# One fused layer on one core: when w_out starts, and how the first expert's products leave PSUM

## The chip, the cores and the metric

One core of a Trainium2 chip runs the whole kernel in one launch. The metric is the device time in microseconds (us). TensorE is PE in the profile, VectorE is DVE, ScalarE is ACT, GpSimd is POOL, and SP issues most of the DMAs.

## The reference

512 tokens with 1024 features go through one layer, all in float32:

```python
h = layer_norm(x)
proj = h @ w_in                       # splits into the inputs of two mixers and two gates
mixed = sigmoid(z_gla) * (gla_branch(...) @ w_gla_proj) + sigmoid(z_fox) * (fox_branch(...) @ w_fox_proj)
h = layer_norm(ALPHA * h + mixed @ w_out)
logits = h @ w_router + b_router      # top 4 of 32 experts for each token, softmax over the four
gu = xb @ w_gate_up[e] + b_gate_up[e] # for the tokens xb of expert e
y = ((clip(up) + 1) * min(gate, 7) * sigmoid(1.702 * gate)) @ w_down[e] + b_down[e]
out = layer_norm(ALPHA * h + sum over the four experts of weight * y)
```

## The kernel before

The work of each engine is one list of instructions written out by hand, with semaphores between the lists. There is no scheduler: an engine that waits holds back all that stands behind it in its list.

Every large product is done in three passes of fp32r matmuls (`passes`, L1694 to L1696): weight and data are each split into a high and a low part, and high x high, high x low and low x high are summed in PSUM. ACT writes the high part of a weight tile (a copy into fp32r), DVE then writes the low part (raw minus high). A weight tile is 128 x 2048 values, 1 MB, and SP loads it with one DMA. Expert weights go through 6 raw buffers and 4 split buffers, tile n of the experts being numbered over all of them: 8 tiles of w_gate_up and 4 of w_down for each expert. SP may load tile n when DVE has split tile n - 6; ACT may split tile n when PE has used tile n - 4; PE may use tile n when DVE has split it.

PSUM has eight banks of 512 columns: `psA` (four) and `psX` (four).

The w_out stage. The last dense product before it, w_fox_proj, has four chunks. A chunk has two halves, each in a bank of `psA`: chunk 38 fills banks 0 and 1, chunk 39 banks 2 and 3. DVE takes each half out with two instructions (L1346, L1347: szf times the bank, added to mix) and counts `dve_half` up; `mix_low` (L1326) writes the low part of mix. After the loop, at L1991, PE waits for all sixteen halves, and then forms `mixed @ w_out` for four token blocks t. Token block t fills two banks, 2(t % 2) and the next. Its four weight tiles j are: j // 2 picks the column half and with it the bank, j % 2 picks which half of the 1024 summed features. Inside t, PE also turns rows of the block before for the router. On DVE `mix_norm(t)` takes the two banks out, adds the residual and normalises; its first instructions also wait for the loads of h and of the norm's gains and offsets, which POOL issues when the dense products are done (L622 to L624).

Routing. Each token block gives a row of lists: `list_row(t)` on DVE (five instructions, L1431 to L1435) writes the places and weights, and `list_tile(t)` on POOL (L647) scatters them with four indirect DMAs into a table in DRAM. When all sixteen have landed, POOL loads the table back (`ltab`, L693); DVE reads it for the first time at L1598, at the end of expert 1. Experts 0 to 3 don't need the table: PE makes their token lists with small matmuls (`table`, L2050), which DVE reads with `take_table`. POOL's queue after the table's load goes on with two loads, the bias rows of expert 2, the gather of expert 3's rows and the scatter of expert 0's results.

Experts. PE's order for expert 0: eight gate-up tiles into all four banks of `psA` (gate in 0 and 1, up in 2 and 3), the bias (`gate_up_bias`, L2105, which raises `gu_done`), and a small table. Then `body(1)`: it waits for `gate_min` and, ahead of bank 2, for `up_ev`, because expert 1's first tile overwrites the same four banks. After tile c = 2 it turns expert 0's activations (`turn_a`), after c = 4 and c = 5 it counts overflow. The down products of expert i - 1 follow the gate-up products of expert i.

DVE's order around it: `swiglu_in(0)` takes the gate banks out with one instruction of 128 x 1024 (L1517), then the up banks with another (L1519); ACT applies Silu; `swiglu_out(0)` (L1525) multiplies. The low parts of expert 1's tiles are written between these: `step_lo(1, c)`.

Of the kernel before, what the change touches and what calls it, by code (L numbers as in the profile page):

```python
# [13 lines left out]
ALU = mybir.AluOpType  # L14
# [8 lines left out]
P = 128  # L23
D = 1024
T = 512
TT = T // P
# [10 lines left out]
LIMIT, SLOPE = 7.0, 1.702  # L37
# [80 lines left out]
def build(nc, a, out):  # L118
# [437 lines left out]
    def _(pool):  # L556
# [86 lines left out]
        def list_tile(t):  # L643

            pool.wait_ge(list_rows, t + 1)
            for k in range(TOPK):
                g.indirect_dma_start(list_dram, bass.IndirectOffsetOnAxis(ap=lidx[:, t, k:k + 1], axis=0),  # L647
                                     lval[:, t, k, :], None, bounds_check=list_bound, oob_is_err=False).then_inc(list_out, 16)

        def gather(tables, turned):  # L650

            if turned is None:
                pool.wait_ge(early_ready, 1)
                pool.wait_ge(lo_ready, NCD + 1)
            else:
                pool.wait_ge(tab_ready, tables)
                pool.wait_ge(xt_done, turned)
            pool.sem_inc(gathers, 1)
            g.indirect_dma_start(xg[:], None, h2_dram, bass.IndirectOffsetOnAxis(ap=gidx[:, 0:1], axis=0),
                                 bounds_check=token_bound, oob_is_err=False).then_inc(xg_in, 16)  # L660
# [22 lines left out]
            g.dma_start(acc_tiles[t], h2[:, t, :]).then_inc(acc_out, 16)  # L683
        pool.wait_ge(list_blank, 16)
        list_tile(0)
        list_tile(1)
        pool.wait_ge(gu_done, 1)
        load_bgu(1)
        gather(3, 2)
        list_tile(2)  # L690
        list_tile(3)
        pool.wait_ge(list_out, 16 * TT * TOPK)
# [66 lines left out]
    def _(act):  # L759
# [280 lines left out]
            s_.copy(dst[:], ps).then_inc(sem, 1)  # L1040

        def silu(i):
            act.wait_ge(gate_min, i + 1)
            s_.activation(act_t[:], gate_t[:], ACT.Silu, scale=SLOPE).then_inc(silu_done, 1)

        def y_evac_over(j, free):
# [95 lines left out]
    def _(dve):  # L1142
# [283 lines left out]
        def list_row(t):  # L1426

            seq.join()
            if t >= 1:
                dve.wait_ge(list_rows, t)  # L1430
            seq.link(v.tensor_tensor(lprod[:], hot[:, t], posm[:, t, 0:E].unsqueeze(1).broadcast_to(shape), ALU.mult))  # L1431
            seq.link(v.tensor_reduce(lpos[:], lprod[:], AX_X, ALU.add))
            seq.mark(v.scalar_tensor_tensor(lidx[:, t, :], lpos[:], float(LE), top_f[:, t, 0:TOPK], ALU.mult, ALU.add))
            seq.link(v.tensor_tensor(lprod[:], hot[:, t], gval[:, t, :].unsqueeze(1).broadcast_to(shape), ALU.mult))
            v.tensor_reduce(lval[:, t, :, 1], lprod[:], AX_X, ALU.add).then_inc(list_rows, 1)  # L1435
# [7 lines left out]
        def step_lo(i, c):  # L1443
            tile_lo(tile_slot(c), tile_no(i, c), c)
# [33 lines left out]
                        ALU.subtract).then_inc(xT_lo_s, 1)  # L1478
        tile_lo(2, 2, 2)
        tile_lo(3, 3, 3)  # L1480
        list_row(1)
        seq.mark(weigh(3))
        seq.join()
        v.tensor_copy(gate_s[:], gate_s[:]).then_inc(vals_ready, 1)
# [8 lines left out]
        def take_table(x, chain):  # L1493

            dve.wait_ge(tab_done, x + 1)
            chain.mark(v.tensor_reduce(queue[:, 3, 1:2], psD[:, 0, 2:4], AX_X, ALU.add))
            if isinstance(x, int) and x <= 1:
                chain.join()
                v.tensor_copy(queue[:, 3, 0:1], psD[:, 0, 0:1]).then_inc(tab_ready, 1)
                dve.wait_ge(tab_ready, x + 1)  # L1500
                return
            dve.wait_ge(xg_in, 16 * (x - 1))
            chain.link(v.tensor_copy(queue[:, 3, 0:1], psD[:, 0, 0:1]))
            chain.mark(v.tensor_scalar(didx[:], queue[:, 0, 0:1], BIG, None, ALU.add))
            v.tensor_scalar(gidx[:], psD[:, 0, 0:1], BIG, None, ALU.add).then_inc(tab_ready, 1)
# [9 lines left out]
        def swiglu_in(i):  # L1515
# [3 lines left out]
            v.tensor_scalar(by_pair(up_t), psA[:, 2:4, :].rearrange("t b (q p k) -> t (b q) k p", p=P, k=2), LIMIT,  # L1519
                            -LIMIT, ALU.min, ALU.max).then_inc(up_ev, 1)  # L1520

        def swiglu_out(i):
            dve.wait_ge(silu_done, i + 1)
            dve.wait_ge(up_ev, i + 1)
            v.scalar_tensor_tensor(act_t[:], up_t[:], 1.0, act_t[:], ALU.add, ALU.mult).then_inc(act_ready, 1)  # L1525
# [6 lines left out]
        tile_lo(0, 6, 6)  # L1532
        tile_lo(1, 7, 7)
        take_table(1, seq)
        for b in range(3):
            ins = v.tensor_copy(member3[:, :, b * E:(b + 1) * E], member[:])
        ins.then_inc(counts_in, 1)
        step_lo(1, 0)
        turned_lo(xT_hi_s, 2, xT1_hi, xT1_lo, xT_lo_s)
        shift_queue(seq)  # L1540
        step_lo(1, 1)
        swiglu_in(0)
        step_lo(1, 2)
        take_table(2, seq)
        swiglu_out(0)
        step_lo(1, 3)
        list_row(2)
        list_row(3)
        seq.join()
        start = seq.used  # L1550

# [136 lines left out]
    def _(pe):  # L1688
# [299 lines left out]
            if t == TT - 1:  # L1988
                ins.then_inc(xt_done, 1)

        pe.wait_ge(dve_half, 2 * (NCD - NPROJ))  # L1991
        pe.wait_ge(wo_lo_s, 4)
        for t in range(TT):
            if t >= 2:
                pe.wait_ge(wo_evac, 2 * (t - 1))
            for j in range(4):
                hi = wo_high(j).rearrange("p (k c) -> p k c", k=HK)
                lo = raw_lo[:, (NCD + j) % RAW, :].rearrange("p (k c) -> p k c", k=HK)
                dst = psA[:, 2 * (t % 2) + j // 2, :]
                for kk in range(HK):  # L2000
                    k = HK * (j % 2) + kk
                    if t == 0 and j < 2:
                        pe.wait_ge(mix_lo_s, k + 1)
                    tok = slice(t * P, (t + 1) * P)
                    ins = passes(dst, (mix_hi[:, k, tok], mix_lo[:, k, tok]), (hi[:, kk, :], lo[:, kk, :]),
                                 k == 0, k == KT - 1)
                if j % 2 == 1:
                    ins.then_inc(wo_done, 1)
                if j == 0 and t >= 2:
                    turn_logits(t - 2)  # L2010
                if j == 2 and t >= 1:
                    turn_h2(t - 1, 0)
                    turn_h2(t - 1, 1)
                if j == 1 and t == 2:
                    positions(0)
                if j == 2 and t == TT - 1:
                    positions(1)
            if t >= 1:
                route(t - 1)
# [54 lines left out]
        def gate_up(n, c, parts, after_first=False):  # L2074

            tile_ready(n)
            hi, lo = xsplit(c)
            for b in range(4):
                if after_first and b == 2:
                    pe.wait_ge(up_ev, 1)  # L2080
                cols = slice(b * 512, (b + 1) * 512)
                ins = passes(psA[:, b, :], (parts[0][:, c, :], parts[1][:, c, :]), (hi[:, cols], lo[:, cols]), c == 0,
                             False)
            ins.then_inc(tile_used, 1)
# [68 lines left out]
        gate_up_bias(0)  # L2153
        pe.wait_ge(tab_ready, 2)
        table(2, 2)

        def body(i):
            first = isinstance(i, int) and i == 1
            second = isinstance(i, int) and i == 2
            split_ready(xT_hi_s, xT_lo_s, i + 1)  # L2160
            if first:
                pe.wait_ge(gate_min, 1)
            else:
                pe.wait_ge(up_ev, i)
            for c in range(GUC):
                gate_up(tile_no(i, c), c, (xT1_hi, xT1_lo) if first else (xT_hi, xT_lo), first and c == 0)
                if first:
                    if c == 2:
                        turn_a(0, 1)
                    if c == 4:  # L2170
                        overflow_counts()
                    if c == 5:
                        overflow_ranks()
                if c == GUC - 2:
                    if first:
                        overflow_list()
                        pe.wait_ge(tab_ready, i + 2)
                        table(i + 2, bass.ds(i + 2, 1))
                if second and c == 3:
                    pe.wait_ge(bd_in, 64)  # L2180
                    pe.wait_ge(tab_ready, 4)
                    pe.wait_ge(y_ready, 1)
                    split_ready(aT_hi_s, aT_lo_s, 2)
                    gate_bias(0)
                if second and c == 5:
                    pe.wait_ge(stage_ready, TT)
                    gate_bias(1)
            gate_up_bias(i)
            if second:
                pe.wait_ge(stage_ready, 2 * TT)  # L2190
            split_ready(aT_hi_s, aT_lo_s, i)
            turn_x(i + 1)
            if first:
                pe.wait_ge(tab_ready, i + 3)
                pe.wait_ge(routed, 1)
            else:
                pe.wait_ge(y_ready, i - 1)
            for q in range(DNC):
                down(tile_no(i, GUC + q), GUC + q, q)
            turn_a(i, i + 1)  # L2200
# [61 lines left out]
```

## Time and profile before

| | us |
|---|---|
| median of 3 runs | 1767.01 |
| lowest, highest of the 3 | 1764.19, 1767.33 |
| the profiled execution | 1764.92 |
| its span | 1763.3 |

| engine | busy, us | share of the span |
|---|---|---|
| PE | 1728.7 | 98% |
| DVE | 1342.0 | 76% |
| ACT | 1114.0 | 63% |
| POOL | 286.3 | 16% |

Times in the rows are us from the start of the span. In a row of the timeline the number in square brackets is how long the engine had been idle before the instruction, with the instruction that ended the wait. Neighbouring instructions of one engine overlap a little, so what one costs in a full queue is the distance from its start to the next start.

### The profile page before, as it was taken

To read this page: it belongs to the slowest core of one execution; us is meant where nothing else is said; L and a number is where in the kernel's file an instruction comes from. 1 tells how busy PE (TensorE), PEld (TensorE's weight loads), DVE (VectorE), ACT (ScalarE), POOL (GpSimd) and SP (SyncE) were. 2 spreads that over 40 slices of the span, in tenths; PEclk is the share of its full clock that TensorE was granted. 3 is DMA by queue.
4 is the path that set the end of the run, shared out by engine and by line. 5 is a ranking of instruction groups with operands and counts; after the bars stand their busy time and mean duration, and the time that the engine had idled before them with its cause. 6 is when DMAs were issued, how large, how long until landed. Compare 5 with 4: busy or idle time off the path is not lost. (4 is left out here: it accounts for less than half of the span.)

```text
span 1763.3 us, 23505 instructions
## 1 busy us (share of the span) xinstructions
PE 1728.7 (98%) x8305; PEld 1408.9 (80%) x8306; DVE 1342.0 (76%) x1172; ACT 1114.0 (63%) x946; POOL 286.3 (16%) x227
## 2 busy tenths in 40 slices
PE   9999999999999999999999999999999999999995
PEld 6777888888887777888788888888888888888884
DVE  6323324333356899998999999999999999999998
ACT  5534334463222567777777777777777777777775
POOL 3000000000001252221212121212121212122211
PEclk9999999999999999999999999999999999999997
DMA  8322322122332699999999999999999999999994
GB/s 295 95 91 72 87 81 67 54 72 88 104 119 97 226 351 385 356 380 379 375 376 377 370 382 374 368 377 385 367 374 380 386 364 371 388 385 362 366 379 165
DMA packets 115697, 487.98 MB, mean 277 GB/s; under 512 B 18912, under 2 KB 49632, under 8 KB 66497
## 3 DMA queue, kind: packets, MB, share of 16 engines
q1 hardware_dynamic: 99576, 455.76, 67.1%
q0 software_dynamic: 16064, 31.55, 6.4%
q8 instruction: 32, 0.52, 0.1%
q14 instruction: 17, 0.13, 0.0%
q10 hardware_dynamic: 8, 0.01, 0.0%
HBM read 476.22 MB, written 28.36 MB: 286 GB/s over the span
## 5 line engine op out<-in xcount | busy, mean ns | idle before, releaser
L1441 DVE TENSOR_TENSOR wlo<-raw,whi 128x2048 fp32r<-128x2048 f32 x382 | 863.3, 2288 | 65.3 <-ACT whi L988 64.2
L988 ACT CAST whi<-raw 128x2048 fp32r<-128x2048 f32 x382 | 724.7, 1913 | 202.3 <-PE psA L1696 165.7
L1694 PE MATMUL psA<-whi,xT_hi 128*128 128x512 f32 x1036 | 408.1, 394 | 2.3 <-issue 2.3
L1695 PE MATMUL psA<-wlo,xT_hi 128*128 128x512 f32 x1036 | 404.3, 390 | 0.0
L1696 PE MATMUL psA<-whi,xT_lo 128*128 128x512 f32 x1036 | 404.2, 390 | 0.0
L1694 PEld LDWEIGHTS psA<-whi,xT_hi 128*128 128x128 f32 x1036 | 195.2, 188 | 43.5 <-issue 4.2
L1696 PEld LDWEIGHTS psA<-whi,xT_lo 128*128 128x128 f32 x1036 | 195.2, 188 | 40.9
L1695 PEld LDWEIGHTS psA<-wlo,xT_hi 128*128 128x128 f32 x1036 | 195.4, 189 | 39.3
L1694 PE MATMUL psX<-whi,aT_hi 128*128 128x512 f32 x496 | 195.8, 395 | 0.0
L1696 PE MATMUL psX<-whi,aT_lo 128*128 128x512 f32 x496 | 193.4, 390 | 0.0
L1695 PE MATMUL psX<-wlo,aT_hi 128*128 128x512 f32 x496 | 193.3, 390 | 0.0
L1162 DVE TENSOR_TENSOR wlo<-raw,whi 128x2048 fp32r<-128x2048 f32 x40 | 92.5, 2311 | 121.4 <-ACT whi L769 121.3
L1694 PE MATMUL psA<-hT_hi,whi 128*128 128x512 f32 x416 | 164.5, 395 | 0.0
L670 POOL DMA_INDIRECT acc_dram<-y_t,didx x31 | 103.5, 3337 | 364.5 <-ACT y_t L1055 279.1
L1696 PE MATMUL psA<-hT_hi,wlo 128*128 128x512 f32 x416 | 162.1, 390 | 0.0
L1695 PE MATMUL psA<-hT_lo,whi 128*128 128x512 f32 x352 | 137.1, 389 | 0.0
L675 POOL DMA_DIRECT2D bgu<-bgu_dram x64 | 38.8, 609 | 480.2 <-PE psA L2105 476.9
L769 ACT CAST whi<-raw 128x2048 fp32r<-128x2048 f32 x40 | 76.5, 1912 | 59.3 <-PE psA L1696 58.6
L1696 PEld LDWEIGHTS psX<-whi,aT_lo 128*128 128x128 f32 x496 | 93.1, 188 | 19.5
L1694 PEld LDWEIGHTS psX<-whi,aT_hi 128*128 128x128 f32 x496 | 93.2, 188 | 18.6 <-issue 0.2
L1695 PEld LDWEIGHTS psX<-wlo,aT_hi 128*128 128x128 f32 x496 | 93.2, 188 | 18.5
L1694 PEld LDWEIGHTS psA<-hT_hi,whi 128*128 128x128 f32 x416 | 78.1, 188 | 17.1 <-issue 1.8
(393 smaller groups left out, 2008.0 us busy)
## 6 DMA issues: line engine op xcount, KB each, us to landing
raw<-in_w_gate_up SPq DMA_DIRECT2D x254, 1024.0 KB, 8.9
raw<-in_w_down SPq DMA_DIRECT2D x128, 1024.0 KB, 8.3
raw<-in_w_in SPq DMA_DIRECT2D x32, 1024.0 KB, 5.4
raw<-in_w_gla_proj SPq DMA_DIRECT2D x4, 1024.0 KB, 5.1
raw<-in_w_fox_proj SPq DMA_DIRECT2D x4, 1024.0 KB, 5.1
raw<-in_w_out SPq DMA_DIRECT2D x4, 1024.0 KB, 5.0
xt<-in_x SPq DMA_DIRECT2D x4, 512.0 KB, 7.1
h_dram<-xt POOLq DMA_DIRECT2D x4, 512.0 KB, 6.1
```

The lines of the kernel that those rows point to most:

```text
L670: g.indirect_dma_start(acc_dram, bass.IndirectOffsetOnAxis(ap=didx[:, 0:1], axis=0), y_t[:], None, bounds_check=token_bound, oob_is_err=Fa ...
L675: g.dma_start(bgu[part:P:32, :], bgu_rows[part, e, :].rearrange("(n c) -> n c", c=512)).then_inc(bgu_in, 16)
L769: s_.copy(whi[:, c % SPL, :], raw[:, c % RAW, :]).then_inc(hi_ready, 1)
L988: s_.copy(xsplit(c)[0], xraw(slot)).then_inc(hi_ready, 1)
L1162: v.tensor_tensor(wlo[:, c % SPL, :], raw[:, c % RAW, :], whi[:, c % SPL, :].bitcast(F32), ALU.subtract).then_inc(lo_ready, 1)
L1441: v.tensor_tensor(lo, xraw(slot), hi.bitcast(F32), ALU.subtract).then_inc(lo_ready, 1)
L1694: mm(dst, sh, mh, start=first, stop=False)
L1695: mm(dst, sh, ml, start=False, stop=False)
L1696: return mm(dst, sl, mh, start=False, stop=last)
```

## The change

Five edits:

1. In the w_out stage PE waits for 14 of the 16 halves before token block 0 (the two of chunk 38 and all before them) and for all 16 before token block 1, and takes block 0's weight tiles in the order j = 0, 2, 1, 3.
2. Expert 0's products leave PSUM by banks: `first_in` takes the place of `swiglu_in(0)`, with four instructions of one bank each. PE's first tile of expert 1 waits for each bank by itself. Silu's count is moved by the two additional signals.
3. `first_in` stands ahead of `step_lo(1, 1)`, where `swiglu_in(0)` stood behind it.
4. `list_row(1)` goes from ahead of `weigh(3)` to the other two list rows, behind `step_lo(1, 3)`; POOL's `list_tile(1)` goes behind the gather of expert 2's rows. The three copies into `member3` go from ahead of `step_lo(1, 0)` to behind `take_table(2)`.
5. PE does four 128 x 128 matmuls of ones behind the table ahead of `body(1)`.

```diff
-        list_tile(1)
         pool.wait_ge(gu_done, 1)
         load_bgu(1)
         gather(3, 2)
+        list_tile(1)
         list_tile(2)
         list_tile(3)
...
-            act.wait_ge(gate_min, i + 1)
+            act.wait_ge(gate_min, 2 if isinstance(i, int) and i == 0 else i + 3)
...
         tile_lo(3, 3, 3)
-        list_row(1)
         seq.mark(weigh(3))
...
+        def first_in():
+
+            dve.wait_ge(gu_done, 1)
+            for b in range(4):
+                src = psA[:, b, :].rearrange("t (q p k) -> t q k p", p=P, k=2)
+                dst = by_pair((gate_t, up_t)[b // 2])[:, 2 * (b % 2):2 * (b % 2) + 2]
+                if b < 2:
+                    v.tensor_scalar(dst, src, LIMIT, None, ALU.min).then_inc(gate_min, 1)
+                elif b == 2:
+                    v.tensor_scalar(dst, src, LIMIT, -LIMIT, ALU.min, ALU.max).then_inc(gate_min, 1)
+                else:
+                    v.tensor_scalar(dst, src, LIMIT, -LIMIT, ALU.min, ALU.max).then_inc(up_ev, 1)
...
         take_table(1, seq)
+        step_lo(1, 0)
+        turned_lo(xT_hi_s, 2, xT1_hi, xT1_lo, xT_lo_s)
+        shift_queue(seq)
+        first_in()
+        step_lo(1, 1)
+        step_lo(1, 2)
+        take_table(2, seq)
         for b in range(3):
             ins = v.tensor_copy(member3[:, :, b * E:(b + 1) * E], member[:])
         ins.then_inc(counts_in, 1)
-        step_lo(1, 0)
-        turned_lo(xT_hi_s, 2, xT1_hi, xT1_lo, xT_lo_s)
-        shift_queue(seq)
-        step_lo(1, 1)
-        swiglu_in(0)
-        step_lo(1, 2)
-        take_table(2, seq)
         swiglu_out(0)
         step_lo(1, 3)
-        list_row(2)
-        list_row(3)
+        for t in range(1, TT):
+            list_row(t)
         seq.join()
...
-        pe.wait_ge(dve_half, 2 * (NCD - NPROJ))
+        pe.wait_ge(dve_half, 2 * (NCD - NPROJ) - 2)
         pe.wait_ge(wo_lo_s, 4)
         for t in range(TT):
+            if t == 1:
+                pe.wait_ge(dve_half, 2 * (NCD - NPROJ))
...
-            for j in range(4):
+            for j in (0, 2, 1, 3) if t == 0 else range(4):
...
-                if after_first and b == 2:
+                if after_first and b == 3:
                     pe.wait_ge(up_ev, 1)
+                elif after_first:
+                    pe.wait_ge(gate_min, b + 1)
...
         table(2, 2)
+        for _ in range(4):
+            mm(psX[:, 1, 2 * P:3 * P], ones[:], ones[:], start=True, stop=True)
...
-            if first:
-                pe.wait_ge(gate_min, 1)
-            else:
+            if not first:
                 pe.wait_ge(up_ev, i)
```

## Rows read from the trace of the kernel before

**Rows 1.** The page, part 1: busy us, share of the span, instructions.

```profile
PE 1728.7 (98%) x8305; PEld 1408.9 (80%) x8306; DVE 1342.0 (76%) x1172; ACT 1114.0 (63%) x946; POOL 286.3 (16%) x227
```

**Rows 2.** Waits of PE: instruction, releaser, us in total, times, longest.

```profile
PE psA L1694 <- issue: 2.3, 2, 1.9
```

**Rows 3.** Windows: length, busy of each engine, granted clock, DMA share, GB/s.

```profile
540.00:542.00 2.00, 0.49 (x4) 0.07 (x2) 1.45 (x3) 0.06 (x2) 0.92 (x2) 1.00 0.00 0
631.00:633.20 2.20, 0.31 (x3) 0.22 (x2) 2.20 (x3) 2.18 (x2) 1.22 (x2) 0.81 1.11 362
633.20:639.20 6.00, 5.97 (x14) 4.74 (x15) 5.97 (x8) 1.90 (x3) 1.24 (x1) 0.50 0.98 351
840.00:876.00 36.00, 34.55 (x160) 28.28 (x158) 32.61 (x21) 26.29 (x17) 10.00 (x5) 1.00 1.01 377
```

**Rows 4.** Timeline where w_out starts: start, us, engine, line, operation.

```profile
535.76 2.29 DVE L1337 TENSOR_TENSOR raw_lo<-raw,wlo 128x2048 fp32r<-128x2048 f32 x1
...
540.10 0.39 PE L1696 MATMUL psA<-hT_hi,wlo 128*128 128x512 f32 x1
...
541.85 1.46 DVE L1326 TENSOR_TENSOR mix_lo<-mix,mix_hi 128x512 fp32r<-128x512 f32 x2
...
541.99 0.50 PE L1694 MATMUL psA<-whi,mix_hi 128*128 128x512 f32 x1 [1.51 <-DVE mix L1347]
```

**Rows 5.** Timeline, DVE's first normalised block and PE's turn of it.

```profile
558.02 0.75 DVE L1388 SCALAR_TENSOR_TENSOR h<-h,small,lnmix_b 128x512 f32<-128x512 f32 x1
...
561.17 1.03 PE L1947 MATMUL psX<-ident,h 128*128 128x128 f32 x8
```

**Rows 6.** Timeline of PE: expert 0's bias, its table, tile c = 4 of expert 1.

```profile
630.26 0.51 PE L2105 MATMUL psA<-bgu,ones_r 2*128 2x512 f32 x4
630.70 0.61 PE L2050 MATMUL psX<-vals,slots 128*128 128x4 f32 x4
...
647.89 0.39 PE L1694 MATMUL psA<-whi,xT_hi 128*128 128x512 f32 x1
```

**Rows 7.** Timeline of DVE from expert 0's last tiles to expert 1's c = 5.

```profile
625.07 0.68 DVE L1536 COPY member<-member 128x128 f32<-128x128 f32 x3
...
629.59 2.29 DVE L1441 TENSOR_TENSOR wlo<-raw,whi 128x2048 fp32r<-128x2048 f32 x1
631.80 1.22 DVE L1517 TENSOR_SCALAR gate_t<-psA 128x1024 f32<-128x1024 f32 x1
...
636.27 0.15 DVE L1496 TENSOR_REDUCE small<-psX 128x1 f32<-128x2 f32 x1
...
636.66 1.22 DVE L1525 SCALAR_TENSOR_TENSOR act_t<-up_t,act_t 128x1024 f32<-128x1024 f32 x1
637.79 2.28 DVE L1441 TENSOR_TENSOR wlo<-raw,whi 128x2048 fp32r<-128x2048 f32 x1
639.99 0.28 DVE L1431 TENSOR_TENSOR lprod<-hot,posm 128x128 f32<-128x128 f32 x1
...
642.67 0.86 DVE L1469 TENSOR_SCALAR slots<-iota,posm 128x128 fp32r<-128x128 f32 x4
...
647.39 1.22 DVE L1510 TENSOR_TENSOR aT_lo<-psX,aT_hi 128x1024 fp32r<-128x1024 f32 x1 [1.66 <-ACT aT_hi L1040]
```

**Rows 8.** Timeline: POOL's list writes and the table's load; DVE's first use.

```profile
641.60 1.05 POOL L647 DMA_INDIRECT list_dram<-lval,lidx  x1 [2.77 <-DVE lval L1435]
...
662.23 0.60 POOL L693 DMA_DIRECT2D ltab<-list_dram  x1 [5.85 <-DMA list_dram<-lval,lidx]
...
680.96 0.17 DVE L1598 CAST lrows<-ltab 128x34 uint32<-128x34 f32 x1
```

**Rows 9.** DMA issues of 640 to 680: count, KB each, median us to landing.

```profile
list_dram<-lval,lidx POOLq DMA_INDIRECT x8, 5.6
ltab<-list_dram POOLq DMA_DIRECT2D x1, 34.0 KB, 6.1
```

**Rows 10.** The same of 605 to 630.

```profile
list_dram<-lval,lidx POOLq DMA_INDIRECT x8, 13.0
```

## The prediction

> **What bounds the kernel now.** I read the busy shares of the page first, then the waits of PE, then windows of a few microseconds around the two places that the change touches, then the timelines there. PE is busy 1728.7 of 1763.3 us [rows 1]: whatever doesn't change when PE works changes nothing. The waits of PE give the few places where it is late [rows 2]. The windows price two of them [rows 3]. From 540 to 542 PE is busy 0.49 of 2.00 us, at full clock. From 631.0 to 633.2 it is busy 0.31 of 2.20 us, and inside that stretch the granted clock begins to fall (0.81, which is 0.84 us at half rate); the next 6.00 us stand at 0.50, that is 1.2 in place of 2.4 GHz, and hold 14 matmuls. At full clock the timeline has matmul starts 0.227 us apart (a tile of 12 is 2.72 us), so 14 take 3.2 us, and the slow stretch costs 2.8 us. Behind it PE stands at 36 of 36 us in most windows, so a microsecond gained or lost at 640 reaches the end. One exception: from 840 to 876 PE lacks some 1.45 us at a DMA share of 1.01 [rows 3]. DMA is full there, but its transfers are released by PE's own progress, six tiles ahead, so an earlier PE starts them earlier; I take this stretch as unchanged.
>
> **The start of w_out.** Before, PE's last matmul of the dense products starts at 540.10 and the first of w_out at 541.99, released by mix at L1347 [rows 4]; the natural next start is 540.33. What PE still needs is there: the last low part of w_out's tiles ends at 538.05, and banks 0 and 1 were emptied for chunk 38, one chunk of 10.9 us earlier. Tiles j = 0 and j = 2 need only the first four parts of mix; 24 matmuls take until 545.8, and the last two low parts of mix end at 543.31 [rows 4]. Saved: 541.99 - 540.33 = 1.66 us. What is late next? Bank 0 of block 0 is now done after 36 matmuls and not 24, at 548.5, but DVE starts that block only when the norm's inputs have come, which is later still. The turn of block 0 on PE moves from 561.17 to 559.51, and DVE starts the second half of that block at 558.02 for 0.75 us, so ends at 558.77 [rows 5]: 0.7 us of cover, and each microsecond by which those inputs come later than here costs one beyond it. From there on all stages up to expert 0's end wait for PE, so they move with it. The bounds of this edit are 0 and -1.66; I take **-1.66**. The times below are those of the old trace, without this shift.
>
> **PSUM by banks.** The bias starts at 630.26 and takes 0.51 [rows 6], so `gu_done` stands at about 630.8. Before, DVE was then in `step_lo(1, 1)` (629.59) and came to the gate banks at 631.80 [rows 7]. Now it comes early: without `list_row(1)` (1.34 us: two rows lie between 639.99 and 642.67) and the member copies (0.7) it is ready at about 627.6, and waits over 3 us for the bias. A bank of 512 columns isn't in the trace of before for this operation; half of 1.22 us is the lower bound, the whole of it the upper, and I take 0.62, next to half, as DVE's rows scale with columns. Gate bank 0 is free at 631.5, the four at 633.3; PE uses a bank for 0.68 us, so it never catches up with DVE inside this tile. The table ends at 631.3 [rows 6], the four ones take 4 x 0.11 (eight 128-column turns take 1.03 [rows 5], with the last one's drain), so PE starts tile 8 at 631.75 in place of 633.2. That is 1.5 us, and with no long gap the clock most likely stays up here, another 2.8.
>
> **But DVE is next, and it loses what PE gains.** In front of tile c = 1 stands `step_lo(1, 1)`, which formerly was done before the evacuation and now comes behind it. DVE's queue, each cost as start to start [rows 7]: four banks to 633.3; c = 1 (2.21, from 629.59 to 631.80) to 635.5; c = 2 to 637.7; the four small table instructions (0.39, 636.27 to 636.66) to 638.1; the member copies, newly here (0.6 to 0.7), to 638.7; `swiglu_out` (1.13) to 639.9; c = 3 (2.2) to 642.1; three list rows where there were two (3 x 1.34 = 4.0) to 646.1; slots (0.8) to 646.9; c = 4 (2.2) to 649.1. PE: c = 0 until 634.5, waits 1.0, c = 1 from 635.55, c = 2 until 641.0, the turn until 641.8, c = 3 from 642.1 to 644.8. Then it waits **4.3 us** for c = 4 and starts it at 649.1. Before, it started c = 4 at 647.89 [rows 6]. So at c = 4 PE is 1.2 us later than before, although it left expert 0 1.5 us earlier and ran at full clock. The reason is the DVE work moved into this stretch: 2.2 + 0.7 + 1.34 = 4.2 us more, +0.2 for two more instructions, less 0.95 of earlier start, less the 1.66 us that DVE formerly waited at aT_lo [rows 7]. That wait is gone, and the low parts of c = 5 follow 3.3 us behind those of c = 4, just PE's own pace with its count. **+1.2**; bounds +0.5 (banks at half cost, every start-to-start a little less) and +1.8 (without a slow clock DVE, now late by 1.7, is also last at expert 1's act_t).
>
> **The clock in the new gap.** PE idle for 1.0 us of 631.0 to 632.4 and hardly loaded just before was enough here for the fall; 1.5 us at 540.5 were not [rows 3, 4]. A gap of 4.3 us is longer than either. The cost: before, the low clock stayed for 6.0 us after PE had resumed, and lost 2.8. If it begins about 1 us into the gap and lasts as long as before, 0.84 + 6.0 = 6.8 us in all, 3.6 us of work at half rate remain, losing 1.7. Nothing covers it, as DVE by then is no longer ahead of PE nor behind it. Between 0 (no fall) and 3.6 (a fall only at the end of the gap) I take **+2.3**, between the two that come from the row of the slow stretch.
>
> The Trainium skill (TensorE: Matmul & The Clock Gate, "Loop structure matters more than you think") says that a copy out of PSUM by DVE between two groups of matmuls leaves PE warm. This trace disagrees: the clock fell during just such a copy, 0.81 in 631.0 to 633.2 and then 0.50. By that rule there would be no fall in either kernel's evacuation; the gap here is at a tile's low part, about which the sentence says nothing.
>
> **Sum.** 1764.92 (the profiled execution; span 1763.3 and 1.6 around it) - 1.66 + 1.2 + 2.3 = 1766.8. That execution lies 2.1 us below the median of the runs, 1767.01; the same change on the median gives 1768.9. The four times of before average 1765.9, which gives 1767.7. I forecast **1768**: no change that a measurement can tell, leaning to slower.
>
> **Lists on POOL: the rival on the slower side.** Instead of eight list writes behind the gather there are twelve, and the first now waits for DVE at 643.5. Eight took from 641.60 to 656.4 [rows 8], 1.85 each, so twelve end at 665.9. POOL then waits for the landings: 5.85 us before [rows 8] gives 671.8; with the 13.0 of the earlier burst [rows 10] it is 678.9. The table's load lands 6.1 later [rows 9]: 677.9 or 685.0. DVE wants it at L1598, 680.96 before [rows 8], now about 682 to 685, and I estimate a tile, some 2.5 us, that PE has in hand there. Behind the load in POOL's queue stand expert 2's bias rows, expert 3's gather and expert 0's scatter, which start 10 to 17 us later than before, all of them needed only when PE is at the end of expert 2. It decides from a landing at about 686 on, and then costs one for one: with writes of 2.1 us and landings of 13 us the table comes at 690 or 691, +4 to +5, so 1771 on the profiled execution and 1773 on the median. For it: the bursts are as slow as that under full DMA. Against: DMA is less full from 642 to 655.
>
> The Trainium skill (DMA: Bandwidth & Descriptors, "Anatomy of one DMA — SWDGE (gpsimd) path") gives about 2 us of fixed cost for a DMA from GpSimd. The trace shows medians of 5.6 and 13.0 us for these list writes [rows 9, 10], so it disagrees. By the page's figure the table would be back by about 671, an estimate, and this rival would have no chance; the measured rows leave it one.
>
> **It does what it says.** If DVE kept up, PE would be at c = 4 at 631.75 + 10.9 + 0.8 = 643.45 and not 647.89: -4.4, with -1.66 it is -6.1, 1758.8 on the profiled execution and 1761 on the median. Against it stands only the sum of DVE's queue, but that has no free stretch: c = 4's low part would have to end 5.6 us before my figure.
>
> **No fall of the clock.** Then only the stalls count: -1.66 + 1.7 = 0, the time of before, 1765 to 1767. For it: the fall in the trace needed more than a gap of 1.5 us, and PE works at full rate before and behind this gap. Against: 4.3 us.
>
> **Chances.** The forecast 0.55, lists late 0.15, as it says 0.08, no fall 0.18, the rest 0.04 for something that I don't see. A measurement of this kernel tells about 0.2%, 3.5 us, from no change. Slower by more than that: the lists and the upper part of the forecast (fall late, or counted from the low runs), 0.27. Faster: 0.09. Within: 0.64. The range 1763 to 1773.5 holds the forecast with both ends of the clock's cost, no fall, and the lists up to +5; it leaves out "as it says".
>
> **What would show it.** w_out's first matmul follows the last dense one by 0.23 us. DVE waits 3 us for PE ahead of `first_in`; four instructions of 0.65 us each; the clock stays at 1.00 from 631 to 640 (less the shift). PE waits about 1.0 us for wlo ahead of c = 1 and over 4 us ahead of c = 4, with the clock at 0.50 behind it. POOL loads the table at 672 or later, without a wait of DVE at L1598. I am wrong if PE reaches c = 4 of expert 1 without that gap, or if the clock stays up through it.

## The result, and the profile after

| | before | after |
|---|---|---|
| median of 22 runs each, us | 1763.85 | 1766.83 |
| lowest to highest | 1762.51 to 1767.33 | 1765.35 to 1769.16 |
| the profiled execution (span) | 1764.92 (1763.3) | 1766.36 (1764.8) |

The ratio of after to before is 1.0016, with a 95% interval of 1.0010 to 1.0022: the change makes the kernel 1.8 to 3.9 us slower. The medians differ by 3.0 us, less than the 0.2% (3.5 us) that the prediction took for the least that a measurement can tell, but with 22 runs each it is outside noise. The first three runs of before (median 1767.01) were high ones; with 22 its median is 1763.85.

The waits of PE in the kernel after (instruction, releaser, us in total, times, longest). Compare [rows 2]:

```profile
PE psA L1706 <- DVE wlo L1441: 4.8, 2, 4.1
PE psX L1713 <- DVE act_t L1537: 1.9, 2, 1.1
...
PE psA L1706 <- issue: 0.3, 1, 0.3
```

The 1.9 us ahead of expert 1 and the wait for mix are gone. (The 0.3 us of "issue" lie behind 900 us; before has the same 0.3 there.) Between 625 and 675 PE now waits for nothing but the new releaser on top: the low part of a weight tile, `wlo`, twice, once for 4.1 us. The windows around those places, columns as in [rows 3]:

```profile
541.00:543.00 2.00, 2.00 (x11) 1.65 (x10) 1.42 (x4) 0.09 (x1) 0.87 (x2) 1.00 0.00 0
629.50:633.00 3.50, 3.50 (x24) 2.96 (x24) 2.87 (x5) 3.31 (x3) 1.22 (x2) 1.00 1.04 377
644.20:648.40 4.20, 0.08 (x1) 0.02 (x1) 4.10 (x11) 1.90 (x1) 3.59 (x3) 0.84 0.44 176
648.40:653.60 5.20, 5.19 (x12) 4.06 (x13) 5.20 (x3) 0.00 (x0) 4.89 (x2) 0.50 0.76 240
840.00:876.00 36.00, 35.29 (x166) 28.78 (x165) 32.63 (x19) 26.21 (x16) 9.09 (x5) 1.00 1.01 378
```

PE is full where w_out starts and where expert 1 starts, at full clock. It is empty from 644.2 to 648.4, and there the granted clock falls to the 1.2 GHz level; the 12 matmuls behind it take 5.2 us at 0.50. Two gaps of before were closed and a larger one was opened behind them.

The start of w_out and the turn of the first block (answers to [rows 4, 5]):

```profile
541.15 0.39 PE L1708 MATMUL psA<-hT_hi,wlo 128*128 128x512 f32 x1
541.38 0.39 PE L1706 MATMUL psA<-whi,mix_hi 128*128 128x512 f32 x1
...
559.19 0.75 DVE L1388 SCALAR_TENSOR_TENSOR h<-h,small,lnmix_b 128x512 f32<-128x512 f32 x1
560.42 1.03 PE L1959 MATMUL psX<-ident,h 128*128 128x128 f32 x8
```

PE between the experts, with the tile that waits (answers to [rows 6]):

```profile
629.50 0.51 PE L2121 MATMUL psA<-bgu,ones_r 2*128 2x512 f32 x4
629.94 0.61 PE L2064 MATMUL psX<-vals,slots 128*128 128x4 f32 x4
630.41 1.14 PE L2173 MATMUL psX<-ones 128*128 128x128 f32 x8
631.30 0.48 PE L1706 MATMUL psA<-whi,xT_hi 128*128 128x512 f32 x1
...
648.41 0.76 PE L1706 MATMUL psA<-whi,xT_hi 128*128 128x512 f32 x1 [4.13 <-DVE wlo L1441]
```

DVE's queue meanwhile (answers to [rows 7]). It waits 3.17 us for the bias and is then without a pause until the low part of c = 4 is done, 645.99 + 2.28:

```profile
630.13 1.29 DVE L1528 TENSOR_SCALAR gate_t<-psA 128x512 f32<-128x512 f32 x2 [3.17 <-PE psA L2121]
...
632.53 4.48 DVE L1441 TENSOR_TENSOR wlo<-raw,whi 128x2048 fp32r<-128x2048 f32 x2
...
637.32 0.49 DVE L1555 COPY member<-member 128x128 f32<-128x128 f32 x3
637.73 1.22 DVE L1537 SCALAR_TENSOR_TENSOR act_t<-up_t,act_t 128x1024 f32<-128x1024 f32 x1
638.87 2.28 DVE L1441 TENSOR_TENSOR wlo<-raw,whi 128x2048 fp32r<-128x2048 f32 x1
641.07 0.28 DVE L1431 TENSOR_TENSOR lprod<-hot,posm 128x128 f32<-128x128 f32 x1
...
645.18 0.88 DVE L1469 TENSOR_SCALAR slots<-iota,posm 128x128 fp32r<-128x128 f32 x4
645.99 2.28 DVE L1441 TENSOR_TENSOR wlo<-raw,whi 128x2048 fp32r<-128x2048 f32 x1
```

POOL's list writes, the table's load and DVE's first use of it (answers to [rows 8, 9]):

```profile
642.68 1.05 POOL L647 DMA_INDIRECT list_dram<-lval,lidx  x1 [2.77 <-DVE lval L1435]
...
672.09 0.98 POOL L647 DMA_INDIRECT list_dram<-lval,lidx  x1 [0.30 <-issue]
676.22 0.60 POOL L693 DMA_DIRECT2D ltab<-list_dram  x1 [3.15 <-DMA list_dram<-lval,lidx]
```

```profile
683.49 0.17 DVE L1610 CAST lrows<-ltab 128x34 uint32<-128x34 f32 x1
```

And the landings of 640 to 680, with the columns of [rows 9]:

```profile
list_dram<-lval,lidx POOLq DMA_INDIRECT x12, 5.1
ltab<-list_dram POOLq DMA_DIRECT2D x1, 34.0 KB, 4.1
```

To follow where time goes, I use one table for all kernels. Its columns are distances of PE's bias rows (L2105 before, L2121 after) in each one's profiled execution: expert 0 to expert 1 (the stretch of the change), 1 to 2, and 2 to 8. Undisturbed, an expert takes 35.02 us, so the last column is 210.1 when PE never waits there. "Clock low" is how long the granted clock was 0.50 between 625 and 660.

| kernel | median, us | ratio to before, interval | bias 0 to 1 | 1 to 2 | 2 to 8 | clock low |
|---|---|---|---|---|---|---|
| before | 1763.85 | 1 | 30.47 | 38.04 | 213.5 | 6.8 |
| after | 1766.83 | 1.0016 (1.0010 to 1.0022) | 34.37 | 37.61 | 212.4 | 6.8 |
| e1_w_out_alone | 1761.76 | 0.9987 (0.9978 to 0.9996) | 29.00 | 38.03 | 212.4 | 3.4 |
| e1b_wait_alone | 1762.94 | 0.9994 (0.9985 to 1.0003) | 28.50 | 38.19 | 213.8 | 0 |
| e2_expert_part_alone | 1768.48 | 1.0021 (1.0012 to 1.0030) | 34.23 | 37.61 | 213.1 | 6.8 |
| e6_old_queue_order | 1761.88 | 0.9985 (0.9976 to 0.9994) | 28.69 | 38.19 | 213.8 | 0 |
| e5b_old_order_no_ones | 1762.24 | 0.9995 (0.9986 to 1.0005) | 28.73 | 38.17 | 212.6 | 0 |
| e3_lo_ahead_of_banks | 1763.79 | 1.0001 (0.9992 to 1.0010) | 29.59 | 38.36 | 216.5 | 0 |
| e11_row1_back | 1764.36 | 1.0003 (0.9994 to 1.0012) | 31.95 | 37.61 | 214.0 | 3.4 |
| e9_ones_in_the_gap | 1767.16 | 1.0017 (1.0008 to 1.0026) | 34.63 | 37.61 | 212.2 | 0 |
| e9b_half_the_ones | 1765.52 | 1.0011 (1.0002 to 1.0020) | 31.87 | 38.59 | 212.7 | 0 |
| e8_member_on_act | 1761.29 | 0.9986 (0.9977 to 0.9995) | 28.13 | 38.17 | 211.9 | 0 |
| e10_before_bias_spread | 1761.63 | 0.9990 (0.9981 to 0.9999) | 28.53 | 38.19 | 210.1 | 0 |
| e12_all_gains | 1758.28 | 0.9966 (0.9954 to 0.9978) | 28.14 | 38.17 | 210.1 | 0 |

The medians of before beside the experiments were 1763.4 to 1764.1.

### The profile page after: what moved, and what is told of

It is laid out like the page before. It is cut to its first block, busy times and chain, and to the rows that moved or that the text cites. A ratio compares the mean times of both kernels' runs of the same rounds, so it can differ in the third digit from the quotient of the medians.

```text
span 1764.8 us, 23552 instructions
## 1 busy us (share of the span) xinstructions
PE 1729.7 (98%) x8313; PEld 1410.7 (80%) x8314; DVE 1342.3 (76%) x1174; ACT 1113.8 (63%) x946; POOL 291.0 (16%) x227
## 4 chain that ended last, share of the span: by engine, by line
PE 90%; DVE 4%; ACT 2%; DMA 2%; issue 2%; POOLq 0%; SPq 0%; DVEq 0%; ACTq 0%
PE psA L1706 21%; PE psA L1708 21%; PE psA L1707 21%; PE psX L1706 6%; PE psX L1708 6%; PE psX L1707 6%; PE psX L1713 3%; DVE wlo L1441 1%; DMA raw<-in_w_down 1%; PE psX L1900 1%; PE psX L1885 1%; ACT whi L988 1%; PE psA L2121 1%; PE psX L1909 0%; DMA raw<-in_w_in 0%
```

## The experiments

**The two halves of the change.** First each alone: w_out's three edits on the kernel before, and the change without them.

```diff
-        pe.wait_ge(dve_half, 2 * (NCD - NPROJ))
+        pe.wait_ge(dve_half, 2 * (NCD - NPROJ) - 2)
         pe.wait_ge(wo_lo_s, 4)
         for t in range(TT):
+            if t == 1:
+                pe.wait_ge(dve_half, 2 * (NCD - NPROJ))
...
-            for j in range(4):
+            for j in (0, 2, 1, 3) if t == 0 else range(4):
```

> The kernel before with the w_out part of the change alone (14 halves, order 0, 2, 1, 3). Theory (the stages behind wait for PE, so the start of w_out reaches the end whole): the first w_out matmul 0.23 us behind the last dense one, expert 0's bias 1.7 us earlier, -1.7 us in all, ratio 0.9990. Rival (the norm's inputs or the routing chain take it back): 0, ratio 1.000.

> The change without its w_out part. Theory: DVE's moved work makes PE wait over 4 us for the low part of c = 4, and the clock falls in that gap; from expert 0's bias to expert 1's bias 34.4 us in place of 30.5, in all +3 to +4.5 us, ratio 1.0017 to 1.0025. Rival (the slowdown comes from w_out starting earlier, which shifts everything against the DMAs): 0 or faster.

Measured 0.9987 and 1.0021, both near what was expected: by these ratios w_out's part gains about 2.3 us and the expert part loses about 3.7 us; by the medians beside those of before in the same session (1763.83) it is 2.1 and 4.6. The product of the ratios, 1.0008, lies a little under the 1.0016 of both together, by no more than their intervals allow; the medians add up to 2.6 of 3.0 us. From the last low part of mix to expert 0's bias it takes 87.6 to 87.7 us with the old start and 85.8 to 85.9 with the new one: 1.8 us, and all of it reaches the bias. One profiled execution with the new start, that of e3, takes 87.5: there the granted clock was 0.50 from 598.8 to 602.0, in a stretch where the code is the same in all kernels and no other profile has a fall. So the loss is in the expert part.

**Is the order of the tiles needed?** The same without the last of the three edits.

> The kernel before with PE's earlier start of w_out (14 halves ahead of block 0, 16 ahead of block 1) in the old tile order 0, 1, 2, 3. Theory (the order isn't needed: tile j = 1 comes 2.7 us behind the start, and its first low part is there, each of the others 0.68 us later): the same 1.7 us as with the new order, ratio 0.9987 to 0.9990. Rival (j = 1 reaches the last parts of mix too early and waits): up to 0.5 us less gain.

From mix to the bias it is 85.85 us, the same as with the new order. The waiting edit is the whole gain in the trace. The measured 0.9994 is compatible with 0.9987, and with no change; this run alone would not show the gain.

**The old order of the queues around the evacuation by banks.** The changed kernel with DVE's and POOL's lists as before:

```diff
+        for b in range(3):
+            ins = v.tensor_copy(member3[:, :, b * E:(b + 1) * E], member[:])
+        ins.then_inc(counts_in, 1)
         step_lo(1, 0)
         turned_lo(xT_hi_s, 2, xT1_hi, xT1_lo, xT_lo_s)
         shift_queue(seq)
+        step_lo(1, 1)
         first_in()
-        step_lo(1, 1)
         step_lo(1, 2)
         take_table(2, seq)
-        for b in range(3):
-            ins = v.tensor_copy(member3[:, :, b * E:(b + 1) * E], member[:])
-        ins.then_inc(counts_in, 1)
         swiglu_out(0)
         step_lo(1, 3)
-        for t in range(1, TT):
-            list_row(t)
+        list_row(2)
+        list_row(3)
...
         tile_lo(3, 3, 3)
+        list_row(1)
         seq.mark(weigh(3))
...
         list_tile(0)
+        list_tile(1)
         pool.wait_ge(gu_done, 1)
         load_bgu(1)
         gather(3, 2)
-        list_tile(1)
```

> The changed kernel with DVE's and POOL's old order around it: list row 1, its list writes, the member copies and the low part of c = 1 stand where they stood before, all ahead of the evacuation by banks. Theory (the 4.2 us of moved DVE work are the loss): DVE comes to the banks 0.95 us behind the bias, PE starts expert 1 at about 632.5 on the old axis, waits about 1.8 us ahead of c = 4 and starts it 1.9 us earlier than in the kernel before; with w_out's 1.7 it is -3.3 us against before, ratio 0.998, and up to 3 us less if the clock stays up. Rival (four small instructions and bank waits are what costs): still slower than before, ratio over 1.000.

Measured 0.9985, 1.9 us under before by the medians: faster than before, as the theory has it, but by less than the 3.3 us expected, although the clock stayed up in the profile. PE's waits from 625 to 675 in this kernel:

```profile
PE psA L1707 <- DVE wlo L1441: 1.3, 1, 1.3
PE psX L1714 <- DVE act_t L1538: 0.4, 1, 0.4
PE psA L1707 <- DVE gate_t L1529: 0.3, 1, 0.3
```

The gap of 4.1 us is gone with nothing changed but the places of DVE and POOL instructions, so the four small instructions and the waits by bank are not the loss. But the second thing that this run shows is against me: expert 0 to 1 takes 28.69 us, and the old evacuation takes 28.50 and 28.53 where the clock happened to stay up (e1b, e10). In these traces taking the banks out one by one gains nothing even in the better order, and the medians of this kernel and of e1, 1761.88 and 1761.76 in one session, say the same. The 1.9 us ahead of expert 1 were DVE being late, not the size of its instruction; with banks PE starts earlier and waits the same time a few tiles later.

**Single moved terms.** The low part of c = 1 alone put ahead of `first_in()`, and list row 1 with its list writes alone put back.

> The changed kernel with the low part of expert 1's c = 1 again ahead of the evacuation by banks, in the 3.2 us in which DVE waits for the bias; list rows, list writes and member copies stay late. Theory (DVE's queue in this stretch is a plain sum, of which this is the largest moved term, 2.2 us): PE doesn't wait ahead of c = 1, and the gap ahead of c = 4 shrinks from 4.5 to about 2.7 us; 2.2 us under the changed kernel, ratio 1.0004, and 2.5 lower still where the clock stays up. Rival (the list rows alone make the gap): less than 0.5 us, ratio 1.0015.

> The changed kernel with list row 1 and its list writes back in their old places, nothing else. Theory (a plain sum): DVE's wait ahead of the banks shrinks from 3.2 to 1.8 us, the gap ahead of c = 4 from 4.5 to 3.2 us, 1.4 us under the changed kernel, ratio 1.0008. Rival (what matters is twelve list writes in one burst on POOL): much more than 1.4 us.

The waits of PE from 625 to 675, e3 first and e11 second:

```profile
PE psA L1706 <- DVE wlo L1441: 2.8, 1, 2.8
```

```profile
PE psA L1707 <- DVE wlo L1441: 3.3, 2, 2.7
```

Of the two waits of e11 one is the 0.6 us ahead of c = 1, as after. The wait ahead of c = 4 went from 4.1 to 2.8 and 2.7 us, where I expected 2.7 and 3.2 (with the 0.2 us between two starts). The medians fell by 3.0 and 2.5 us, where I expected 2.2 (more if the clock stays up) and 1.4. In the traces expert 0 to 1 is 4.8 and 2.4 us shorter: 2.2 and 1.4 from the queue, the rest from a fall of the clock that is gone in e3 and half as long in e11. A plain sum over DVE's queue fits, and e11's 2.5 us need no cost of the twelve list writes of their own. The profiled execution of e3 took 1768.0, the upper end of its runs, with the fall of the clock at 598.8 and 216.5 us from expert 2 to 8; its median is 1763.79.

**What the clock costs.** PE was given matmuls of ones inside the gap:

```diff
             for c in range(GUC):
+                if first and c == 4:
+                    for _ in range(32):
+                        mm(psX[:, 1, 2 * P:3 * P], ones[:], ones[:], start=True, stop=True)
```

> The changed kernel with 32 more 128 x 128 matmuls of ones on PE between c = 3 and c = 4 of expert 1, into an unused stretch of PSUM: some 3.5 us of work inside the gap of 4.5 us. Theory (the fall of the clock in the gap costs 2.3 to 2.8 us of its own): the granted clock stays at 1.00 there and the time is 2.5 us under the changed kernel, ratio to before about 1.000. Rival (the slow stretch is covered by DVE's queue): no difference from the changed kernel, 1.0016.

The time was that of the changed kernel, 1.0017. That was not the rival, but my size: the 32 lasted 7.3 us, and c = 4 started at 651.50 in place of 648.41. The clock stayed up. So with 16:

> As the kernel with ones in the gap, but with 16 matmuls: in the earlier run each 128 x 128 float32 matmul took two passes, 0.23 us, so that 32 of them lasted 7.3 us and pushed c = 4 back by 3.1 us, as much as the clock gave. 16 take 3.6 us, inside the gap of 4.5. Theory (the fall costs 2.5 us by itself): the clock stays at 1.00, c = 4 starts when its low part is done, 2.5 us under the changed kernel, ratio 1.0002. Rival (DVE's queue covers the slow stretch): 1.0016 as before.

Windows of that kernel, the old gap and what follows it:

```profile
644.20:647.60 3.40, 3.40 (x32) 3.35 (x31) 3.33 (x9) 1.90 (x1) 2.79 (x3) 1.00 0.38 153
648.30:653.60 5.30, 5.30 (x28) 4.45 (x29) 5.30 (x3) 1.92 (x1) 5.00 (x2) 1.00 0.72 229
```

5.3 us now hold 28 matmuls where 5.2 held 12. Expert 0 to 1 falls from 34.37 to 31.87, 2.5 us, the price of the fall where it happens. But 1 to 2 rises from 37.61 to 38.59: PE comes to the turn of act_t and to expert 2 ahead of DVE and waits there, 0.3 and 0.4 us, where the changed kernel doesn't wait between 660 and 700. Net 1.5 us in the traces, 1.3 in the medians. Both theories were half right: the fall has a price of its own, and DVE's queue takes back part of it.

**Do the four ones ahead of expert 1 keep the clock up?** The kernel with the old queue order, without them:

> The kernel with the old queue order and the evacuation by banks, without the four matmuls of ones ahead of expert 1. Theory A (the ones keep the clock up): the gap behind the table grows from 0.3 to 1.2 us and the clock falls in it, for 3.4 to 6.8 us as in the kernels without ones; 1.4 to 2.8 us over the kernel with ones, less 1.3 us that DVE's wait ahead of c = 4 hides, so ratio to before 0.9988 to 0.999. Theory B (a gap of 1.2 us is short enough): no fall, same time as with ones, 0.9985, or 0.1 us less.

No fall, with PE empty for 1.4 us, and 28.73 us from expert 0 to 1 against 28.69. In this one trace theory B holds. It is not shown for the kernel: the intervals of 0.9995 and 0.9985 overlap, but each execution, profiled or not, also has a mean granted clock, rounded to 0.001 (0.001 is 3.5 us at the low level), and it is 0.995 in ten of the eleven executions with the ones and in five of the eleven without them. Theory A may hold in some executions. In the kernels with the old evacuation, whose wait of 1.9 us is the same in all four, the fall came in two of four profiled executions: 6.8 us in before, 3.4 in e1, none in e1b and e10. Windows of two of these, the wait and what follows it, e1 first, then e1b. (The Trainium skill, TensorE: Matmul & The Clock Gate, "Loop structure matters more than you think", says that a copy out of PSUM leaves PE warm, in a loop whose next matmuls follow at once. Here PE waited 1.9 us for the copy, and it stayed warm in two of these four and not in two.)

```profile
630.70:632.60 1.90, 0.03 (x1) 0.06 (x1) 1.90 (x3) 1.88 (x2) 1.00 (x2) 0.85 1.07 347
632.60:635.40 2.80, 2.80 (x7) 2.22 (x8) 2.80 (x2) 1.47 (x2) 0.00 (x0) 0.50 0.98 232
```

```profile
630.20:632.00 1.80, 0.00 (x0) 0.01 (x1) 1.80 (x3) 1.78 (x2) 0.95 (x2) 1.00 1.04 402
632.00:638.00 6.00, 5.98 (x26) 4.98 (x27) 5.97 (x8) 3.60 (x4) 1.24 (x1) 1.00 1.00 325
```

**Taking work out of DVE's queue, and the waits between 800 and 912.** The first kernel is that of the old queue order, with the member copies on ACT:

```diff
         turned_hi(xt_done, 2, xT1_hi, xT_hi_s)
-        for c in range(1, XSPL):
-            step_hi(1, c)
+        step_hi(1, 1)
+        step_hi(1, 2)
+        act.wait_ge(mem_ready, TT)
+        for b in range(3):
+            ins = s_.copy(member3[:, :, b * E:(b + 1) * E], member[:])
+        ins.then_inc(counts_in, 1)
+        step_hi(1, 3)
         silu(0)
```

> The kernel with the old queue order and the evacuation by banks, with the three member copies on ACT, between its parts of c = 2 and c = 3, in place of DVE. Theory (every 1 us taken out of DVE's queue between 606 and 675 is 1 us of PE's waits, as long as PE waits ahead of c = 4 and at the turn of act_t): DVE 0.6 us earlier at the banks and at c = 4, 0.5 us under the kernel with the copies on DVE, ratio to before 0.9983. Rival (ACT's parts come later by 0.8 us and PE waits for them): same or slower.

Expert 0 to 1 fell from 28.69 to 28.13, as expected; the medians, 1761.29 and 1761.88, differ by the same 0.6 us, which their intervals don't resolve.

The second is the kernel before with the four bias scatters spread; the third has all.

```diff
-            if isinstance(i, int) and 3 <= i < 3 + TT:
-                add_bias(i - 3, i)
+            if isinstance(i, int) and 3 <= i < 3 + 3 * TT and i % 3 == 0:
+                add_bias(i // 3 - 1, i)
...
-        for i in range(1, 3 + TT):
+        for i in range(1, 3 * TT + 1):
             body(i, False)
-        with pool.Fori(3 + TT, E - 2) as i:
+        with pool.Fori(3 * TT + 1, E - 2) as i:
```

> The kernel before with the four scatters of the down-bias rows (0.5 MB each, added in DRAM) issued during experts 3, 6, 9 and 12 in place of 3, 4, 5 and 6. Theory (these four in a row fill the DMA engines and cause PE's 2.1 to 3.9 us of waits between 800 and 912): most of it goes, -2 us or more, ratio 0.9985 to 0.9990. Rival (the DMAs are full there from the weights alone, or each scatter costs its own wait wherever it stands): 1.000.

> w_out's early start, the evacuation by banks in the old queue order, the ones, the member copies on ACT, and the bias scatters spread over experts 3, 6, 9 and 12. Theory (the parts add up, as they act at different places of a PE-bound run): -1.8 (w_out) -0.3 to -1.8 (banks) -0.5 (copies) -2 to -3 (spread) = -4.6 to -7, ratio 0.9965 to 0.9974. Rival (a gain ahead of 660 is taken back by the full DMAs behind it): no better than the spread alone.

Windows of before, of e10 and of e12, in this order:

```profile
800.00:912.00 112.00, 109.33 (x510) 89.07 (x508) 102.88 (x66) 82.91 (x50) 23.60 (x14) 1.00 1.00 375
```

```profile
800.00:912.00 112.00, 112.00 (x529) 91.83 (x529) 104.82 (x64) 84.07 (x51) 26.51 (x16) 1.00 0.99 382
```

```profile
800.00:912.00 112.00, 112.00 (x530) 91.83 (x529) 105.25 (x64) 83.05 (x51) 27.45 (x16) 1.00 0.98 381
```

The ratios are 0.9990 for e10, the upper end of what I expected, and 0.9966 for e12. The waits are gone, and not because the DMA engines have air: their share is 0.99 and 0.98. What changed is the time from issue to landing of the weight tiles. Issues of 800 to 840, before and then e10 (count, KB, median us to landing):

```profile
raw<-in_w_gate_up SPq DMA_DIRECT2D x9, 1024.0 KB, 12.7
raw<-in_w_down SPq DMA_DIRECT2D x4, 1024.0 KB, 12.7
```

```profile
raw<-in_w_gate_up SPq DMA_DIRECT2D x10, 1024.0 KB, 10.1
raw<-in_w_down SPq DMA_DIRECT2D x4, 1024.0 KB, 8.3
```

e12 is the best version found, 0.9966 with an interval of 0.9954 to 0.9978: 3.9 to 8.1 us under the kernel before, and faster than both kernels of this case. Its parts nearly add up: by the medians 2.1 for w_out, 0.6 for the copies and 2.5 for the spread are 5.2 of 5.8 us, inside the 4.6 to 7 expected. It has only six runs.

## Why the prediction was right

**The start of w_out** was -1.66; the trace has 1.8 us and the part alone 2.1 in the medians. The turn of the first block kept 0.5 us of cover, 0.7 foreseen: DVE ended at 559.94, and PE turned at 560.42 without a wait.

**DVE is next.** The sum over DVE's queue gave PE's start of c = 4 at 649.1, 18.84 us behind the bias; measured 648.41 - 629.50 = 18.91. The idle time ahead of it was 4.3 us, measured 648.41 - 643.89 - 0.23 = 4.29. The wait ahead of c = 1 was 1.0, measured 0.8. DVE's wait for the bias was "over 3 us", measured 3.17. The four banks took 2.4 us of queue (630.13 to 632.53) where I had 2.5. One price was wrong by a factor of two without effect: the four ones took 0.9 us and not 0.44, because a float32 matmul of this shape is two rows of the trace, which the turns that I had taken for a measure are not; c = 0 started 0.3 us later and its bank waits hid behind that.

**The clock.** I took +2.3, in place it was 2.5. The low level lasted 6.8 us, as assumed, but began 2.8 us into the gap and not 1, so that 5.5 us of work ran at half rate and not 3.6; the value between my bounds covered that. The upper bound itself should have been half of 6.8 us, 3.4, not 3.6. And I wrote that nothing covers it, and expert 1 to 2 gave back 1.0 (e9b): without the fall DVE is last again behind expert 1. I had this only as an upper bound on the term of DVE's queue.

**The sum** was +1.9 on the profiled execution, measured +1.44, with the stretches: w_out -1.8; expert 0 to 1 +3.9 (predicted 3.5); 1 to 2 -0.4; 2 to 8 -1.0; the tail -0.2; and +1.1 that the profiled execution after was later before w_out began, where the two kernels are the same. The medians differ by 3.0, so there the step was 1.1 too small. The base was too high: I put it between 1764.9 and the 1767.0 of three runs, near 1766, and 22 runs give 1763.85. The two errors have opposite signs, and that the forecast 1768 comes within 1.2 of the 1766.83 measured is in part luck; the mechanism, the waits and their places are not. "No change that a measurement can tell" did not hold: 22 runs tell it.

**The step that was weaker than it looked** is the fall of the clock ahead of expert 1, which I booked as a sure cost of before. It is not one: it came in two of four profiled executions with that wait. In the profiles where it doesn't come, expert 0 to 1 is about 1.9 us shorter than in before, and the change that much worse. The mean granted clocks of the single executions fit this as the reason why the medians differ by more than the two profiles. The profiled execution of before has 0.993. Of its 94 executions beside the experiments 76 have 0.994 or 0.995, with medians of 1763.5 and 1763.6; 12 have 0.993 (1764.8) and 6 have 0.992 (1767.0, the level of the first runs). The changed kernel never has 0.995: eleven times 0.994, ten times 0.993, once 0.992. The five kernels in whose profiles PE waits at most 1.3 us at a time between 625 and 675 (e6, e8, e9, e9b, e12) have 0.995 in 42 of 50 executions; e1b, e10 and e3, with waits of 1.9 to 2.8 us and no fall there in their profiles, in 6 of 33. So the profile of before was one of its slower executions. Where the clock was low in the unprofiled ones is not known, and every profile also has 18 to 22 us at the low level behind 1740, where PE runs out of work; that the difference lies ahead of expert 1 is argued, not shown.

**The rivals.** Lists late: the twelve writes took 30.4 us (642.68 to 673.07) and not 22, under the load that I had named, and the table's load was issued at 676.22, 14 us later than before, in the range given. DVE's first use at 683.49 shows no wait, so its price was zero: 7.3 us were in hand for a landing of 4.1. (The some 2 us of fixed cost that the Trainium skill, DMA: Bandwidth & Descriptors, "Anatomy of one DMA — SWDGE (gpsimd) path", gives for a DMA from GpSimd are too few here too: 5.1 and 4.1.) "It does what it says" is refuted, and in e6 the old order of the queues doesn't bring it about either: PE still waits 1.3 us ahead of c = 4. No fall of the clock: it fell; e9b, where it was kept up by force, is that case, 1765.52, in the range of 1765 to 1767 that I gave. The DMAs from 840 to 876: I took that stretch as unchanged, and its waits (2 to 8 minus 210.1) are 1.8 to 3.9 us in all kernels with the old scatters, e3's profiled execution aside, with no order by how early PE comes; unchanged on average, but not a constant.

## What to carry to other kernels

Before an engine's wait is shortened, add up the queue of the engine that releases it: if that has no idle time up to the next wait, the wait only moves, and whatever work is moved into that stretch in exchange makes it longer. A gap in PE that closes is worth a look at the place where the moved instructions went, not at the place that closed. And when DMAs are full, spreading traffic that isn't urgent can help without removing a byte: what matters is how late the needed tile lands. A single profiled execution can be an unusual one of its kernel: look at where it lies among the others, by time and by mean clock, before its details are booked as costs.

## What the runs showed of the hardware that I had not expected

The same wait of 1.9 us let the granted clock fall in two of four executions, for 6.8 and 3.4 us, and a wait of 2.8 us (e3) in none, one of 2.7 (e11) for 3.4 us; both gaps of 4.1 us (after, e2) had a fall of 6.8 us. Nor does the fall come at one place: it began 1.0 us (before), 1.3 us (e1) and 2.8 us (after) behind the end of the work ahead of the gap, and in e11 1.0 us after PE had taken up work again. With waits of 1.9 to 2.8 us the clock differed from execution to execution.

A 128 x 128 float32 matmul of ones on TensorE is two rows of 0.11 us each, start to start; a turn (transposing matmul) of the same shape is one.

DMA engines at a share of 0.98 to 1.02 don't by themselves make PE wait: at 0.98 PE was full for 112 us (e12), at 1.00 it lacked 2.7 (before). The median landing time of a 1 MB tile between 800 and 840, 8.3 and 10.1 us (e10) against 12.7 (before), tells them apart.
